# Loads of x and of the conditioning weights in turn, and another order of work in the first spot of an encoder layer

## What is computed

```python
mod = jax.nn.silu(c) @ ada_w[l] + ada_b[l]            # c: one row of 1024 per group, ada_w: 1024 x 9216
sh1, sc1, g1, sh2, sc2, g2, sh3, sc3, g3 = jnp.split(mod, N_MOD, axis=-1)
h = modulate(rmsnorm(x, ffn1_norm[l]), sh1, sc1)      # h * (1 + scale) + shift
x = x + 0.5 * g1[:, None, :] * swiglu(h, ffn1_wg[l], ffn1_wu[l], ffn1_wd[l])   # D_FF = 2816
# then token mixing (windowed and latent attention), a second SwiGLU, a last rmsnorm
```

## Time and profile before

| | us |
|---|---|
| median of 3 runs | 2986.58 (2986.42 to 2987.47) |
| the profiled execution | 2986.62 |
| its span | 2984.8 |
| PE busy | 2869.9 (96%) |
| POOL busy | 2231.1 (75%) |
| DVE busy | 1742.5 (58%) |
| ACT busy | 1553.8 (52%) |
| first product of the first spot starts | 78.82 |
| sixth product of the first spot starts | 112.88 |

### The profile page before, as it was taken

How to read it: one execution, slowest core, us unless ns; L and a number is a source line. 1 busy time by engine, 2 the same in 40 slices (tenths; PEclk the granted TensorE clock), 3 DMA queues, 4 the chain that set the end, 5 groups by cost and what they waited for, 6 DMA issues and landing times. The chain is left out here.

```text
span 2984.8 us, 49320 instructions
## 1 busy us (share of the span) xinstructions
PE 2869.9 (96%) x16057; PEld 2643.6 (89%) x16057; DVE 1742.5 (58%) x3002; ACT 1553.8 (52%) x2585; POOL 2231.1 (75%) x1116
## 2 busy tenths in 40 slices
PE   6899999999999999997999999999999999999998
PEld 3899999999999988885666667989999999999998
DVE  5666777767777657876543332274544467544545
ACT  6534444544444467766767775453444355444444
POOL 0788888889888853234557666678898888889884
PEclk9999999999999999998999999999999999999999
DMA  8333233333433335556322235441222232122224
GB/s 283 104 97 117 90 114 100 109 129 99 127 96 116 120 138 146 140 157 153 103 58 77 73 96 158 115 127 57 86 63 77 76 122 99 57 85 63 77 73 160
DMA packets 378610, 323.46 MB, mean 108 GB/s; under 512 B 22780, under 2 KB 325743, under 8 KB 378479
## 3 DMA queue, kind: packets, MB, share of 16 engines
q1 hardware_dynamic: 375342, 320.21, 35.4%
q10 hardware_dynamic: 3136, 1.57, 0.2%
HBM read 263.29 MB, written 58.43 MB: 108 GB/s over the span
## 5 line engine op out<-in xcount | busy, mean ns | idle before, releaser
L2389 POOL TENSOR_TENSOR W_lo<-quart,W_hi 128x1024 fp32r<-128x1024 f32 x384 | 941.8, 2471 | 178.4 <-ACT W_hi L2383 178.1
L2852 PE MATMUL PS<-SL,W_hi 128*128 128x384 f32 x2112 | 715.6, 339 | 31.7 <-issue 16.5
L2854 PE MATMUL PS<-SL,W_lo 128*128 128x384 f32 x2112 | 709.8, 336 | 0.0
L2853 PE MATMUL PS<-SL,W_hi 128*128 128x384 f32 x2112 | 709.7, 336 | 0.0
L2383 ACT ACTIVATE W_hi<-quart 128x1024 fp32r<-128x1024 f32 x384 | 402.9, 1060 | 561.8 <-PE PS L2918 245.0
L2054 DVE SCALAR_TENSOR_TENSOR XT<-PS,mod,XT 128x384 f32<-128x384 f32 (+1 forms) x840 | 418.4, 527 | 271.9 <-PE PS L2918 169.5
L2852 PEld LDWEIGHTS PS<-SL,W_hi 128*128 128x128 f32 x2112 | 399.3, 189 | 40.3 <-issue 24.0
L1844 POOL TENSOR_TENSOR XT_r<-XT,XT_r 128x512 fp32r<-128x512 f32 x224 | 286.9, 1286 | 179.0 <-ACT XT_r L1696 178.6
L2853 PEld LDWEIGHTS PS<-SL,W_hi 128*128 128x128 f32 x2112 | 399.3, 189 | 1.0 <-issue 1.0
L2854 PEld LDWEIGHTS PS<-SL,W_lo 128*128 128x128 f32 x2112 | 399.0, 189 | 0.0
L2411 POOL TENSOR_TENSOR quart<-quart 128x1024 f32<-128x1024 f32 x128 | 317.2, 2478 | 10.4 <-DVE qsum L2411 1.2
(11 more groups left out here) (314 smaller groups left out, 6385.9 us busy)
## 6 DMA issues: line engine op xcount, KB each, us to landing
quart<-in_ffn_wg SPq DMA_DIRECT2D x176, 256.0 KB, 3.1
quart<-in_ffn_wu SPq DMA_DIRECT2D x176, 256.0 KB, 3.4
quart<-in_ffn_wd SPq DMA_DIRECT2D x160, 256.0 KB, 3.0
ada_r<-in_ada_w SPq DMA_DIRECT2D x128, 192.0 KB, 2.5
raw<-in_w_out SPq DMA_DIRECT2D x30, 512.0 KB, 3.9
ada_w_sb<-in_ada_w SPq DMA_DIRECT2D x6, 2048.0 KB, 19.2
XT<-scr_xt SPq DMA_DIRECT2D x8, 1536.0 KB, 8.6
scr_xt<-XT SPq DMA_DIRECT2D x4, 2688.0 KB
```

The source lines that it names most:

```text
L2389: pool.tensor_tensor(W_lo[:, slot_of(S, u), :], unit_src(u), W_hi[:, slot_of(S, u), :].bitcast(F32), ALU.subtract) \
L2852: pe.matmul(out, w_hi, m_hi, start=j in PRODUCT_OPENS and kp == 0, stop=False, skip_group_check=True)
L2853: pe.matmul(out, w_hi, m_lo, start=False, stop=False, skip_group_check=True)
L2854: mm = pe.matmul(out, w_lo, m_hi, start=False, stop=kp == 3, skip_group_check=True)
```

## The change

**Loads.** SP loads four tiles of x, block 0, four tiles, block 1, four tiles, blocks 2 and 3. Block 3 comes in two halves with a semaphore each. `x_in` lies elsewhere, so that blocks can be split while x is still worked on. PE multiplies block 0 before it turns tiles 4 to 7, and block 1 (and turns block 0) before it turns tiles 8 to 11. ScalarE and VectorE take tiles and blocks in the same turn.

**First spot.** `gate_row` moves out of W_lo. The wait for `ada_turned` 6 goes from GpSimd's low part of unit 2 to VectorE's T4, whose room `gate_row` now shares. GpSimd makes the low parts of units 1 and 2 between its sums. ScalarE makes all four shifts, then the high part of unit 1, and only later the two copies of `gate_row`, with the high part of unit 2 between them. The high part of T3 comes after that of unit 3. VectorE makes the low part of T2 before T3.

```diff
-        s1 = ExitStack()
         XR = 4
-        x_in = sb(s1, "x_in", [P, XR, D])
-        s1.close()
...
-        gate_row, = placed(HW + 20480, [("gate_row", [2, 2, CH], F32)])
+        gate_row, = placed(HW + 53248, [("gate_row", [2, 2, CH], F32)])
...
+        x_in, = placed(HW + 24576, [("x_in", [P, XR, D], F32)])
...
         def ada_block_load(sp, b):
             half, c = ada_home(b)
+            if b == 3:
+                for k, landed in ((0, ada_landed[3]), (KD // 2, ada_tail)):
+                    sp.dma_start(ada_w_sb[:, half, k:k + KD // 2, c, :], ada_src[:, k:k + KD // 2, b * CH:(b + 1) * CH])                       .then_inc(landed, 16)
+                return
...
-            for t in range(NT):
-                x, r = (io["x_prompt"], t * P) if t < S_PROMPT // P else (io["x_sample"], t * P - S_PROMPT)
-                if t >= XR:
-                    sp.wait_ge(x_turned, 2 + t - XR + 1)
-                    sp.wait_ge(x_summed, t - XR + 1)
-                sp.dma_start(x_in[:, t % XR, :], x[0, r:r + P, :]).then_inc(x_landed[t % XR], 16)
-            for b in range(4):
-                ada_block_load(sp, b)
+            for c in range(NCH):
+                for t in range(c * TPC, (c + 1) * TPC):
+                    x, r = (io["x_prompt"], t * P) if t < S_PROMPT // P else (io["x_sample"], t * P - S_PROMPT)
+                    if t >= XR:
+                        sp.wait_ge(x_turned, 2 + t - XR + 1)
+                        sp.wait_ge(x_summed, t - XR + 1)
+                    sp.dma_start(x_in[:, t % XR, :], x[0, r:r + P, :]).then_inc(x_landed[t % XR], 16)
+                ada_block_load(sp, c)
+            ada_block_load(sp, 3)
...
             x_turn(pe, 0)
+            pe.wait_ge(silu_ready, 2)
+            ada_block(pe, 0)
             x_turn(pe, 1)
             spread_pe(pe, 0)
             spread_pe(pe, 1)
-            x_turn(pe, 2)
-            pe.wait_ge(silu_ready, 2)
-            ada_block(pe, 0)
             ada_block(pe, 1)
             ada_turn(pe, 0)
+            x_turn(pe, 2)
...
-            x_sums(act, 0)
-            x_sums(act, 1)
-            spread_act(act, 0)
-            spread_act(act, 1)
-            x_sums(act, 2)
             for b in range(4):
+                if b < NCH:
+                    x_sums(act, b)
+                if b == 1:
+                    spread_act(act, 0)
+                    spread_act(act, 1)
                 ada_split_hi(act, b, 0)
...
             op_shift_act(act, 0, B21)
+            op_shift_act(act, 0, B22)
+            spot_hi(act, Spot(GA, 0, 0), 1)
+            op_hi_act(act, 0, B21)
             ada_keep(act, 4)
-            op_shift_act(act, 0, B22)
+            op_hi_act(act, 0, T1)
+            spot_hi(act, Spot(GA, 0, 0), 2)
             ada_keep(act, 5)
-            op_hi_act(act, 0, B21)
             spread_act(act, 2)
             spread_act(act, 3)
-            spot_hi(act, Spot(GA, 0, 0), 1)
-            op_hi_act(act, 0, T1)
-            spot_hi(act, Spot(GA, 0, 0), 2)
             op_hi_act(act, 0, T2)
-            op_hi_act(act, 0, T3)
...
             op_lo_dve(dve, 0, T1)
+            op_lo_dve(dve, 0, T2)
             op_t_dve(dve, 0, T3)
-            op_lo_dve(dve, 0, T2)
             op_lo_dve(dve, 0, T3)
...
             if h == 0 and j == T4:
                 dve.wait_ge(sq_used, 2 + NT)
+                dve.wait_ge(ada_turned, 6)
...
         def spot_lo(pool, S, u):
             pool.wait_ge(unit_hi, S.unit(u + 1))
-            if S.first and S.h == 0 and u == 2:
-                pool.wait_ge(ada_turned, 6)
...
-                spot_lo(pool, S, 2)
+                if not (S.first and S.h == 0):
+                    spot_lo(pool, S, 2)
...
             if f == 0:
-                for no in range(3):
-                    spot_sum(pool, S0, no)
                 spot_lo(pool, S0, 1)
+                spot_sum(pool, S0, 0)
+                spot_lo(pool, S0, 2)
+                spot_sum(pool, S0, 1)
+                spot_sum(pool, S0, 2)
...
                 if S.first and S.h == 0:
-                    for j in (T4, B22):
+                    for j in (T3, T4, B22):
                         op_hi_act(act, 0, j)
```

More of the change, by code:

```diff
@@ L386, in build @@
         raw_kept, RAW0, t_made, MADE0 = diag_ready, NT, x_inv, NCH
-        xt_parked, PARK0 = rows_landed, 16 * len(row_plan)
+        ada_tail, TAIL0 = rows_landed, 16 * len(row_plan)
+        xt_parked, PARK0 = rows_landed, TAIL0 + 16
         xt_unparked, BACK0 = [consts_landed, ada_landed[5]], 16
@@ L796, in ada_split_hi @@
                 act.wait_ge(ada_landed[b], 16)
+            if b == 3 and p == 2:
+                act.wait_ge(ada_tail, TAIL0 + 16)
             if 4 * b + p >= AH // 2:
@@ L878, in start_dve @@
             dve.tensor_tensor(c_hl[:, :, 2:4], silu_c[:, :, :], c_hl[:, :, 0:2].bitcast(F32), ALU.subtract).then_inc(par_ready, 1)
-            x_keep_dve(dve, 0)
-            spread_dve(dve, 0)
-            x_keep_dve(dve, 1)
-            spread_dve(dve, 1)
-            x_keep_dve(dve, 2)
-            spread_dve(dve, 2)
             for b in range(4):
+                if b < NCH:
+                    x_keep_dve(dve, b)
+                    spread_dve(dve, b)
                 for p in range(KD // 2):
```

## The result

| | before | after |
|---|---|---|
| median | 2987.47 (5 runs, 2986.42 to 2990.71) | 3001.87 (5 runs, 2997.86 to 3004.01) |
| the profiled execution | 2986.62 | 3001.87 |
| its span | 2984.8 | 3000.1 |
| ratio, 95% interval | | 1.0043 [1.0033, 1.0054] |

By the ratio the change makes the kernel slower by 12.8 us, with an interval of 9.9 to 16.1 (the two medians lie 14.4 apart). A second set of runs of the same two kernels gave 2997.28 against 2984.85, ratio 1.0042 [1.0029, 1.0056]. The forecast was +9.0: the sign was right, the size too small, and 3001.87 lies 0.9 above the upper end of the stated range. Most of what was missing is in the start, where PE took blocks at half clock.

A forecast was written before the change was run, and what follows sets the result against it. PE, busy 96% of the span, was taken as the bound, so delays before the first spot's sixth product move the end: 2.9 us from the start plus 6.1 from the spot, 2986.62 + 9.0 = 2995.6, range 2989.5 to 3001.0.

The forecast's parts named there:

- the start: The stretch up to the copy of block 3, paced by loads before the change; forecast to end 2.9 us later.
- K: Moment of ScalarE's copy of block 3, which ends the start; 60.06 us before, forecast 63.0.
- A price read from a stretch in which PE ran at full clock: In the start, PE was taken to end a block 2.6 us after its last split, read from block 3 before.
- H: Mark behind the first spot, not itself forecast: start of PE's first matmul that takes `hid`; 151.10 us before.

The follow-up runs named there:

- sums first: The changed kernel with GpSimd's three sums ahead of the low parts of units 1 and 2; ratio 1.0024 [1.0015, 1.0033] against the kernel before.

## What to carry to other kernels

In strictly ordered queues, look at what stands *behind* each wait: the three sums needed only data that lay ready, and low parts put in front of them and between them cost 8.1 us (the changed kernel against sums first). When two engines slow each other down, removing a wait of one can cost more than it gives; look at what the other does at that time before you fill the gap. A load that comes sooner is worth something only if the engines that consume it aren't held up by it: with the same loads in turn, K came 5.0 us later or 5.3 us sooner than before, by the order of one engine. A price read from a stretch in which PE ran at full clock did not hold here for the same work behind a gap.

## What the hardware showed that was not expected

- ScalarE's first split, as soon as a 2 MB block issued at 7.6 us had landed, came between 18.7 and 20.9 in nine executions with loads in turn. With PE's blocks in front of its tiles, K follows it by 44.6 to 45.9 us.
- The same sixteen matmuls of block 1 took PE 5.8 to 6.5 us behind a gap (granted clock 0.50 in most of them) and 3.95 us behind work (1.00).
- VectorE's low part of 128 x 1536 took 1.7 us alone (three in 5.08) and 3.9 beside GpSimd (three in 11.68), in the same kernel but for two instructions' places.
- The first product after 8.5 us in which PE did little started at half clock. In the changed kernel by stretches (the granted clock stands behind the engines' busy times):

```profile
84.00:90.00 6.00, 1.72 (x8) 1.71 (x9) 1.00 (x1) 3.83 (x6) 4.83 (x3) 0.50 0.00 0
90.00:96.00 6.00, 5.51 (x23) 5.22 (x22) 6.00 (x3) 1.32 (x3) 5.92 (x3) 0.73 0.00 0
96.00:102.00 6.00, 6.00 (x36) 6.00 (x36) 6.00 (x2) 1.07 (x1) 4.68 (x3) 1.00 0.00 0
```

- H - K repeats within 0.15 us from execution to execution (91.04 and 90.95, 97.72 and 97.59), while the whole varies by 5 us and more. Two marks close to the change can settle what a median over many runs leaves open there; they don't tell the whole time.
